# Token buffers 32 bytes further on, and a top-k that works in PSUM, in a two-block mixture-of-experts and attention kernel

## What is computed

```python
for l in range(2):
    xn = rmsnorm_2(x, norm_mix[l])
    (qa, ka, va, qb, kb, vb, qc, kc, vc, qi, ki, wi, gates) = jnp.split(xn @ w_in[l], offsets, axis=-1)
    o_a = chunk_band_attention(...)
    o_b = diff_attention(...)
    o_c = dsa_attention(...)          # the index scores below pick 64 keys for each query
    y = g0 * (o_a @ w_up_a[l]) + g1 * (o_b @ w_up_b[l]) + g2 * (o_c @ w_up_c[l])
    x = x + y @ w_out[l]
    x = x + memory_cross_attention(...)
    x = x + swiglu(rmsnorm_2(x, norm_ffn[l]), w_gu[l], w_down[l])

# in dsa_attention, per chunk of queries:
logits = jnp.einsum('bqhd,bsd->bqhs', qi, k_idx) * D_IDX ** -0.5
score = jnp.einsum('bqhs,bqh->bqs', jax.nn.relu(logits), wi)      # 4 index heads
score = jnp.where(admissible, score, -inf)
vals, idx = lax.top_k(score, 64)
```

## Time and profile before

| | us |
|---|---|
| median of 3 runs | 1656.08 (1655.14 to 1656.25) |
| profiled execution | 1649.91 |
| its span on the core | 1647.9 |
| PE busy in the span | 1578.0 (96%) |
| VectorE busy | 893.7 (54%) |
| ScalarE busy | 651.2 (40%) |
| mean granted TensorE clock, share of full | 0.983 |

### The profile page before, as it was taken

One profiled execution on the slowest core, in us unless ns is written; L12 is line 12 of the kernel. 1 busy time (PEld: TensorE's weight loads), 2 busy tenths in 40 slices (PEclk: granted clock), 3 DMA queues, 4 the chain that ended last, 5 costly groups with the idle time before them and its releaser, 6 DMA issues.

```text
span 1647.9 us, 25666 instructions
## 1 busy us (share of the span) xinstructions
PE 1578.0 (96%) x10931; PEld 1274.2 (77%) x10931; DVE 893.7 (54%) x1302; ACT 651.2 (40%) x1022; POOL 62.2 (4%) x30
## 2 busy tenths in 40 slices
PE   9998989899889999999999999999999999999998
PEld 7786434334344359889899799999989889899998
DVE  6933212112121158667886676647566879486654
ACT  2034112112111135455654654435454664554443
POOL 0000000000000000033000000000006000000000
PEclk9988999999999999999999999999999999999999
DMA  9155999999999995636243656474635443275550
GB/s 350 58 238 211 426 430 427 428 430 428 428 430 427 426 377 192 215 109 199 103 154 103 203 164 196 155 258 161 211 120 168 157 154 128 96 227 170 174 204 27
DMA packets 126913, 393.79 MB, mean 239 GB/s; under 512 B 4320, under 2 KB 60000, under 8 KB 114016
## 3 DMA queue, kind: packets, MB, share of 16 engines
q1 hardware_dynamic: 126816, 392.38, 63.0%
HBM read 386.34 MB, written 1.05 MB: 235 GB/s over the span
## 4 chain that ended last, share of the span: by engine, by line
PE 74%; DMA 11%; DVE 11%; ACT 2%; issue 1%; SPq 0%; DVEq 0%; ACTq 0%
PE psum L1259 11%; PE psum L990 10%; PE psum L993 10%; PE psum L991 10%; DMA ring<-w 9%; PE psum L1324 3%; DVE outs L1984 3%; PE psum L1596 2%; PE psum L1594 2%; PE psum L1597 2%; DVE w_lo L636 2%; PE psum L1222 2%; PE psum L951 1%; PE psum L1416 1%; PE psum L1417 1%; PE psum L1021 1%
## 5 line engine op out<-in xcount | busy, mean ns | idle before, releaser
L990 PE MATMUL psum<-h_hi,w_hi 128*128 128x256 f32 x1472 | 366.2, 287 | 0.0
L991 PE MATMUL psum<-h_hi,w_lo 128*128 128x256 f32 x1472 | 360.8, 283 | 0.0
L636 DVE TENSOR_TENSOR w_lo<-raw_a,w_hi 128x1024 fp32r<-128x1024 f32 x184 | 221.9, 1222 | 122.5 <-ACT w_hi L1616 121.9
L990 PEld LDWEIGHTS psum<-h_hi,w_hi 128*128 128x128 f32 x1472 | 281.9, 192 | 5.8 <-issue 5.1
L991 PEld LDWEIGHTS psum<-h_hi,w_lo 128*128 128x128 f32 x1472 | 282.1, 192 | 0.2
L1616 ACT ACTIVATE w_hi<-raw_a 128x1024 fp32r<-128x1024 f32 x202 | 210.3, 1053 | 166.3 <-PE psum L993 68.9
L993 PE MATMUL psum<-h_lo,w_hi 128*128 128x256 f32 x1472 | 206.4, 283 | 0.0
L1259 PE MATMUL psum<-ring,outs 128*64 128x512 f32 x720 | 166.5, 618 | 26.6 <-DMA ring<-w 25.4
L993 PEld LDWEIGHTS psum<-h_lo,w_hi 128*128 128x128 f32 x1472 | 189.9, 192 | 0.0
L1259 PEld LDWEIGHTS psum<-ring,outs 128*64 128x64 f32 x720 | 57.8, 143 | 132.7 <-issue 132.6
L1616 ACT ACTIVATE w_hi<-raw_b 128x1024 fp32r<-128x1024 f32 x100 | 104.6, 1054 | 94.9 <-PE psum L993 56.0
(11 more groups left out here) (311 smaller groups left out, 2544.2 us busy)
## 6 DMA issues: line engine op xcount, KB each, us to landing
ring<-w SPq DMA_DIRECT2D x76, 2048.0 KB, 16.6
raw_a<-w_in SPq DMA_DIRECT2D x20, 2048.0 KB, 8.2
raw_a<-w_gu SPq DMA_DIRECT2D x32, 1024.0 KB, 7.8
raw_b<-w_in SPq DMA_DIRECT2D x10, 2048.0 KB, 8.9
wp<-w SPq DMA_DIRECT2D x8, 2048.0 KB, 18.4
hs<-w SPq DMA_DIRECT2D x8, 2048.0 KB, 22.7
raw_b<-w_gu SPq DMA_DIRECT2D x12, 1024.0 KB, 7.2
raw_a<-w_down SPq DMA_DIRECT2D x8, 1536.0 KB, 6.8
```

The lines of the kernel that those rows point to most:

```text
L636: return eng.tensor_tensor(chunk_part(w_lo, n), chunk_raw(n), chunk_part(w_hi, n).bitcast(F32), ALU.subtract)
L990: mm(to, hi[:, k, :], h_hi[:, k, :], start=(k == 0), stop=False)
L991: mm(to, lo[:, k, :], h_hi[:, k, :], start=False, stop=False)
```

## The change

Three edits. **Placement:** `h_hi` and `h_lo` become views of one tensor `h_parts`, which has 8 elements (32 bytes) ahead of them and 8 behind. They now begin at bytes 50336 and 58528; every tensor behind them moves by 64 bytes (`raw_a` to 66752, `act_parts` to 145056), and `w_lo` and `w_hi` stay. Rows of `h_hi`, `h_lo` and of `act_parts` then all begin 32 bytes past a whole number of 512 from the blocks of weights. The one-column tensors `side` and `eps2` move into unused columns of `lam`. **Top-k:** the last of the four multiply-adds writes its row into the PSUM place of the first head's logits, and the maxima, the replacements and the mask work there; the duo is freed after the mask. **Order:** the 256-column row goes first on ScalarE and VectorE, and ScalarE's first relu waits for both products.

```diff
+H_SHIFT = 8
...
-        + [("index", 0), ("index", 1), ("proj", 9, "qc"), ("proj", 10, "kc"), ("evac", 3, "qc"), ("evac", 4, "kc"),
+        + [("index", 1), ("index", 0), ("proj", 9, "qc"), ("proj", 10, "kc"), ("evac", 3, "qc"), ("evac", 4, "kc"),
...
-        h_hi = sb("h_hi", [P, KD, SEQ], F32R)
-        h_lo = sb("h_lo", [P, KD, SEQ], F32R)
+        h_parts = sb("h_parts", [P, 2 * KD * SEQ + 2 * H_SHIFT], F32R)
+        h_hi, h_lo = (view(h_parts, H_SHIFT + i * KD * SEQ, KD, SEQ) for i in range(2))
...
-        side = sb("side", [P, 1])
-        eps2 = sb("eps2", [P, 1])
+        side, eps2 = lam[:, 4:5], lam[:, 5:6]
...
                     elif kind == "index_product":
-                        t = w[1]
+                        t = 1 - w[1]
                         nk = P * (t + 1)
-                        act_e.wait_ge(idx_done, l * 2 + t + 1)
+                        act_e.wait_ge(idx_done, l * 2 + 2)
...
                     elif kind == "index":
                         t = w[1]
                         nk = P * (t + 1)
-                        v.wait_ge(relu_ready, l * 2 + t + 1)
-                        sc = score[:, 0:nk]
+                        v.wait_ge(relu_ready, l * 2 + 2 - t)
                         logits = view(duo(f"i_{t}"), 0, 4, SEQ)
+                        sc, part = logits[:, 0, 0:nk], score[:, 0:nk]
                         for h in range(4):
-                            add = c("mask")[:, SEQ - nk:SEQ] if h == 0 else sc
-                            link(v.scalar_tensor_tensor(sc, logits[:, (h % 2) * 2 + h // 2, 0:nk], wi[:, t, h:h + 1], add,
+                            add = c("mask")[:, SEQ - nk:SEQ] if h == 0 else part
+                            link(v.scalar_tensor_tensor(sc if h == 3 else part, logits[:, (h % 2) * 2 + h // 2, 0:nk], wi[:, t, h:h + 1], add,
                                                         ALU.mult, ALU.add))
-                        v.sem_inc(free_of(f"i_{t}"), 1)
-
                         for _ in range(TOPK // 8):
                             v.sem_inc(held, 1)
                             link(v.max(top8[:], sc))
                             v.sem_inc(held, 1)
                             link(v.match_replace(sc, top8[:], sc, TAKEN))
                         v.tensor_scalar(selneg[:, t, 0:nk], sc, TAKEN / 3, NEG, ALU.is_gt, ALU.mult).then_inc(selneg_ready, 1)
-                        v.wait_ge(selneg_ready, l * 2 + t + 1)
+                        v.wait_ge(selneg_ready, l * 2 + 2 - t)
+                        v.sem_inc(free_of(f"i_{t}"), 1)
```

## The result

| | before | after |
|---|---|---|
| time, median of the runs side by side, us | 1655.61 (1654.61 to 1656.25) | 1638.88 (1638.12 to 1642.76) |
| profiled execution, its span, us | 1649.9, 1647.9 | 1638.12, 1636.1 |
| start of PE's 2968th matmul, six ahead of the first over the token parts, us | 605.1 | 605.3 |
| second block: from there to PE's last start, us | 1037.3 | 1025.3 |

The account below looks back on a forecast made before the run. PE's matmul distance was taken to bound the second block: 8.4 us from token matmuls plus 0.5 from v projections, sum 8.8, less 0.9 held up, other edits 0, net 7.9; 1656.1 - 7.9 = 1648.2 us, range 1641 to 1657.

Parts of the forecast that it names:

- What bounds the kernel: Second block: time is the number of PE matmuls times the distance between their starts, plus a few waits.
- Step 1: Second block, token parts moving: 118.3 ns instead of 120 at the new place, 5232 x 1.6 ns = 8.4 us gained.
- Step 2: 1440 matmuls over `act_parts`, from 32 bytes short to 32 past: no change, 0, bounds -2.3 to +4.8 us.
- Step 3: 288 v projections, tokens loaded as weights: the same 1.6 ns gained each, 0.5 us.
- Step 4: Gate chunks between attention units: half of their 1.8 us saving lost to PE's waits for VectorE, -0.9 us.
- Step 5: Index stage, row order and top-k in PSUM: VectorE begins 1.5 us later, covered by idle time; cost 0.
- B: Rival, chance 0.08: new place better than that of `act_parts`, all 6960 matmuls at 116.7 ns; 18.2 us less, 1637.9.
- A: Rival, chance 0.17: the operands' place makes no difference to matmul distance; gain 0, time 1656.1 us.
- D: Rival, chance 0.05: VectorE's index stage delays PE in units 8 and 9, 2 us per layer; 1652.2 us.

## Why the prediction was wrong

**What bounds the kernel: right.** The distance between matmuls gave 16.1 us, 4.1 were lost between them, and the index stage took 22.1 us, 0.2 less than before.

**Step 1, the price of the new place: wrong, and the main miss.** "I take 118.3 ns for it, a gain of 1.6 ns each." Measured 116.8 (116.85 where 119.88 stood), a gain of 3.0, which is 15.9 us over 5232 instead of 8.4. The sign and the cause were right; the size came from the row that I had called the nearest. Nearness in bytes means nothing here: 112 gives 113.7, and 96 and 128, 16 away, give 120.0 and 118.6. The lower bound I had written, 116.7, was the value.

**Step 2, `act_parts` 32 past: wrong by 2.4 us.** "By the same reading that is no change, 0". It gained 1.6 ns each. 32 short and 32 past are not mirror images: by themselves they give 118.3 (224) and 116.7 (32).

**Step 3, v projections: wrong in sign.** 0.5 us of gain was forecast; 227.2 became 233.2, 1.7 us of loss. The table shows the role turned has a pattern of its own.

**Step 4, what is held up: too small.** 0.9 us was forecast, and 4.1 measured, of 16.1. I had taken only the gate chunks ahead of VectorE's wait as covered. Pauses grew in places that had none before (`up`, above), each too short to head a list of waits, and 1.4 us is the lower clock of layer 2's cross-attention, for which the sum had no term.

**Step 5, order and top-k: 0, right as a number and wrong as a reason.** VectorE was to begin 1.5 us later and began 1.96 later in the kernel without the placement. A maximum costs 5 ns more and a replacement 13, within the bounds, and the mask costs less. But "None of it reaches the end" holds only where the placement is not there. With it, the mask's read from PSUM is worth 20 us, for without it the kernel is slower than before. The row to doubt was the mask's 774 ns: 1.7 times the time of its neighbour with twice the columns, in the middle of GpSimd's run. I noted that it "may come down" and left it.

**The rivals.** B is what happened. Its 1637.9 against a measured 1638.88 is closer than its working: it counted the v projections as 288 x 3.2 = 0.9 us of gain where they lost 1.7, and 1.8 us as held up where 4.1 were, and stood on a time of before 6.2 us above the profiled one, while after the two are 0.8 us apart. A is excluded; its page rule, "TensorE: Matmul & The Clock Gate" of the Trainium skill, section "Step-by-step: what each phase is for", that weight loads take nothing from the moving reads, leaves no room for distances that go from 113.5 to 121.6 ns by the start of one operand against the other. That the two reads are what gets in each other's way is not shown; the runs show only that the distance goes by the two starts. D did not happen in the change, but in the placement alone it did, by a mechanism that I had not named: not 65 ns for each of 36 instructions but 12.5 us for one. The chance of 0.08 for B was too small. The range had been cut off inside the bounds that I had worked out for the one term that carried everything.

## What to carry to other kernels

Where PE is the bound, treat the start bytes of weights and moving operand against each other as something to tune: measure some ten or twenty starts with a kernel of bare matmuls, since neighbours don't predict one another. Read the bytes at which the tensors really begin from the built program, since padding can put them elsewhere. And check the real kernel, since a run can settle into a slower series. Where VectorE and GpSimd work at the same time, look for a VectorE instruction from SBUF to SBUF that lasts longer than its columns say, and try it with its input in PSUM. Don't price edits one by one when one of them moves the time at which another's instruction meets a busy neighbour.

## What the hardware showed that I had not expected

- The distance between `fp32r` matmuls of 256 columns, with nothing but the operands' addresses changed, lies between 113.4 and 121.6 ns, repeats with 256 bytes at the four places tried twice, and goes by the difference of the two starts (both moved by 64 bytes: 119.8; weights alone: 113.5).
- The steady distances form short series (three or eight matmuls), and one place can have two of them: 113.4 and 117.8 ns at 192 bytes, the latter held over 936 matmuls.
- One mask of 128 columns from SBUF, 0.23 us where nothing holds it, took 12.77 us beside GpSimd's instructions and was let in only when GpSimd had a pause of 0.2 us. In two kernels with the same code for it, it was let in after 0.80 and 0.87 us, just behind the end of one GpSimd instruction.
- After a pause of PE of 1.5 us the granted clock fell in one kernel and not in another whose order of work is the same; after 4.27 us it fell, and 22 matmuls ran at 213 ns.
